# Writing out the loops of three engines, and laying high and low parts side by side, in a two-layer encoder step

## The chip, the cores and the metric

The kernel runs on one core of one Trainium2 chip. The metric is the device time of one launch in microseconds (us), taken as the median of several runs. A core has five engines with instruction streams of their own: TensorE (PE, matrix products; its weight loads are shown apart as PEld), VectorE (DVE), ScalarE (ACT), GpSimd (POOL) and SyncE (SP). They meet through semaphores. The work memory of a core has 128 partitions; products are summed up in PSUM, which has 8 banks here called `ps`.

## What is computed

Two layers for 288 rows of width 2048 (256 of a prompt, 32 of a sample with a past of 512). Each layer normalizes, projects, attends in two ways with 8 heads each, projects back, and ends with a squared-ReLU MLP whose hidden width is 8192. Cut to what matters:

```python
def trunk(x, caches_even, caches_odd):
    for i in range(DEPTH):                       # DEPTH = 2
        h = rms_norm(x, attn_norm[i])
        y, st = even_mixer(h, ...) if i % 2 == 0 else odd_mixer(h, ...)
        x = x + y
        x = x + squared_relu_mlp(rms_norm(x, mlp_norm[i]), w_up[i], w_down[i])

def squared_relu_mlp(h, w_up, w_down):
    return jnp.square(jax.nn.relu(h @ w_up)) @ w_down

def even_mixer(h, ...):
    aq, ak, av, iq, ik, iw, bq, bk, bv, bf = split_cols(h @ w_in, EVEN_SIZES)
    ...
    y = jnp.concatenate([out_a, out_b], axis=-1) @ w_out
```

All of it is in float32. The large products are with weights, 756 chunks of 512 KB of them in all, each read once.

## The kernel before

**Products in three.** A float32 product is made of products of a narrower type (fp32r). A weight chunk is split into `w_high` (a rounded copy, by ScalarE, line 784) and `w_low` (the rest, by VectorE, line 1063), an activation in the same way into `x_high` and `x_low`, or for the MLP's hidden values `hid_high_a`, `hid_low_a` (tiles 0 to 7) and `hid_high_b`, `hid_low_b` (tiles 8 to 15). TensorE then adds high times high (line 352), low activation times high weight (353) and high activation times low weight (354), each a 128x128 weight load and 288 moving columns, into one PSUM tile.

**Groups and chunks.** The weights come as one stream of 189 groups, each 2048 rows by 256 columns, cut into 4 chunks of 128x1024 (512 KB). A group is 96 such products, a chunk 24. The function `group` (from line 340) of TensorE waits per chunk for `low_ready`, and at the group's start for the evacuation of the bank used before. `raw` holds 4 chunks as they landed, `w_high` and `w_low` hold 2 each. For each chunk SyncE starts the load once VectorE has used the chunk 3 earlier; ScalarE makes `w_high` and VectorE `w_low` once TensorE has used the chunk 2 earlier. Between chunks, VectorE also empties the bank of the group before: times the norm factor into `proj` (line 1080), ReLU and square (1105, 1108) and the low part of the hidden values (1113) in an MLP's upper half, or added to `resid` (1124) in its lower half. ScalarE writes the high part of the hidden values (788).

**Order of the phases.** Input projection A (8 groups), a narrow group, projection B (12) with attention A beside it, output projection (16 groups of half length) with attention B beside it, MLP 0 (64 groups), projection C (12), projection D (12) with attention C beside it, output projection with attention D beside it, MLP 1 (64 groups). Work that stands beside attention has been written out in Python. The rest runs in hardware loops (`Fori`), whose bodies TensorE, ScalarE and VectorE pass through again by a branch:

- TensorE: `pairs` (line 388) has a body of two groups: 3 passes in projection A, 5 in projection C. `mlp` (line 411) writes quarter 0 out and has a body of one quarter, 16 groups (8 up, 8 down), for quarters 1 to 3: 3 passes per MLP.
- ScalarE: `plain` (817) one group per pass; projection A two groups (1016); the MLP's quarters 1 and 2 (1036, 1044), with 0 and 3 written out.
- VectorE: `phase_in` (1151) and projection A (1502) two groups; the MLP's quarters 1 and 2 (1531, 1542).

In a loop, the values that are waited for depend on the loop's counter, so register instructions stand between the others. I call the branch from a body's end back to its start a back edge. TensorE has four of a quarter (two per MLP) and six of two groups (two in projection A, four in projection C). SyncE's own loop over all groups stands in both kernels.

Of the kernel before, what the change touches and what calls it, by code (L numbers as in the profile page):

```python
# [11 lines left out]
F32R = mybir.dt.float32r  # L12


P = 128
# [6 lines left out]
H = 8  # L22
# [109 lines left out]
def build(nc, ins, outs):  # L132
    with ExitStack() as ctx:
# [16 lines left out]
        x_high = sb("x_high", [P, KT, T], F32R)  # L150
        x_low = sb("x_low", [P, KT, T], F32R)
# [7 lines left out]
        hid_high_a = sb("hid_high_a", [P, H, T], F32R)  # L159
        hid_low_a = sb("hid_low_a", [P, H, T], F32R)  # L160
# [136 lines left out]
        def _(pe):  # L297
# [84 lines left out]
            def pairs(base, count, moving, first_ready=None, apart=False, lead=0, window=None):  # L382
                group(base, base % 2, moving, ready=first_ready, apart=apart, lead=lead, window=window)
                if apart:

                    pe.wait_ge(mean_ready, 1)
                group(base + 1, (base + 1) % 2, moving, apart=apart, lead=lead)
                with pe.Fori(1, count // 2) as i:
                    group(base + i * 2, base % 2, moving, apart=apart, lead=lead)
                    group(base + 1 + i * 2, (base + 1) % 2, moving, apart=apart, lead=lead)  # L390
# [8 lines left out]
            def mlp(base, name, lead, i_norm):  # L399
# [11 lines left out]
                with pe.Fori(1, QUARTERS) as q:  # L411
                    quarter(q)
# [361 lines left out]
        def _(act):  # L774
# [40 lines left out]
            def plain(base, count, i_norm):  # L815
                body(base, i_norm=i_norm)
                with act.Fori(1, count) as i:
                    body(base + i)
# [197 lines left out]
            with act.Fori(1, IN_A // 2) as i:  # L1016
                for u in range(2):
                    body(i * 2 + u)
                    low_copy(i * 2 + u, u)
# [16 lines left out]
            with act.Fori(1, QUARTERS - 1) as q:  # L1036
                mlp_quarter(G_MLP0, E_OUT0, 0, q)
# [6 lines left out]
            with act.Fori(1, QUARTERS - 1) as q:  # L1044
                mlp_quarter(G_MLP1, E_OUT1, 1, q)
# [4 lines left out]
        def _(dve):  # L1050
# [97 lines left out]
            def phase_in(base, count, i_norm):  # L1148
                evac_in(base, base % 2, 0, i_norm)
                evac_in(base + 1, (base + 1) % 2, 2)  # L1150
                with dve.Fori(1, count // 2) as i:
                    evac_in(base + i * 2, base % 2, i * 4)
                    evac_in(base + i * 2 + 1, (base + 1) % 2, i * 4 + 2)
# [348 lines left out]
            with dve.Fori(1, IN_A // 2) as i:  # L1502
# [28 lines left out]
            with dve.Fori(1, QUARTERS - 1) as q:  # L1531
                quarter(G_MLP0, E_OUT0, 0, q)
# [9 lines left out]
            with dve.Fori(1, QUARTERS - 1) as q:  # L1542
# [295 lines left out]
```

How the kernel before makes its waits and increments, by code:

```python
        @block.sync  # L280
        def _(sp):
            w = ins["w"]
            for kk in range(CH):
                sp.dma_start(raw[:, kk, :], w[kk, :, :]).then_inc(landed[kk], 16)
                sp.dma_start(resid[:, CK * kk:CK * kk + CK, :], ins["x"][:, CK * kk:CK * kk + CK, :])\
                  .then_inc(x_landed[kk], 16)
            with sp.Fori(1, NG) as n:
                for kk in range(CH):
                    sp.wait_ge(low_ready, n * CH + (kk - 3))
                    sp.dma_start(raw[:, kk, :], w[bass.ds(n * CH + kk, 1), :, :].rearrange("a p c -> p (a c)"))\
                      .then_inc(landed[kk], 16)
# [10 lines left out]
            def out_pair(base, lead, half, j, window=None):  # L304
                e = base + lead + OUT_G * half + j
                pe.wait_ge(evacuated, e - 1)
                for i in range(HALF_CH):
                    c = base * CH + (OUT_G * half + j) * HALF_CH + i
                    pe.wait_ge(low_ready, c + 1)
# [14 lines left out]
            def out_half(base, lead, half, before, window=None, windows=0):  # L325
                pe.wait_ge(hid_low_ready, before)
                for j in range(OUT_G):
                    out_pair(base, lead, half, j, window)
                for w in range(OUT_WINDOWS, windows):
                    window(w)
# [28 lines left out]
            def sum_squares(i):  # L360
                pe.wait_ge(sum_ready, POOL_PAIRS + 8 * i)
                out = ps[:, 6 if i == 0 else 4, 0:T]
                if i == 0:
                    pe.wait_ge(sem("dim_squares"), 1)
```

## Time and profile before

| | us |
|---|---|
| median of 3 runs | 2697.96 |
| lowest and highest run | 2697.1, 2708.48 |
| span of the profiled execution | 2695.6 |
| TensorE busy | 2648.1 |
| VectorE busy | 1443.7 |
| ScalarE busy | 996.7 |

The span goes from the first to the last instruction of the profiled execution; its own time is not known apart, and the median lies 2.36 us above its span. In a timeline, a row of the view is its start, its duration, the engine, the line of the kernel, the operation, the tiles and, in brackets, how long the engine had been idle before and who ended that. Durations of products overlap, since they are pipelined: what counts is the distance from one start to the next. "issue" as the ender of an idle time means that nothing the profile shows was waited for.

### The profile page before, as it was taken

The numbers are of one execution on the slowest core, as the hardware profiler recorded it, in microseconds if no ns is written. First come the engines' busy times: TensorE is split into PE (matmuls) and PEld (weight loads), VectorE is DVE, ScalarE is ACT, GpSimd is POOL, SyncE is SP. The second block draws the span as 40 slices with busy tenths as digits, with TensorE's granted clock in tenths as the row PEclk, the third lists the DMA queues.
The fourth block names the chain that finished last, engine by engine and source line by source line (L and its number), as shares of the span: only waits on it lengthen the run. The fifth ranks groups of instructions, "written<-read, shape, count | busy, mean of one in ns | idle before, by whom it ended". The sixth has DMA issues, their size and how long they took to land.

```text
span 2695.6 us, 48256 instructions
## 1 busy us (share of the span) xinstructions
PE 2648.1 (98%) x19365; PEld 2588.9 (96%) x19365; DVE 1443.7 (54%) x1630; ACT 996.7 (37%) x1233; POOL 172.8 (6%) x162
## 2 busy tenths in 40 slices
PE   7999999999999999999999999999999999999998
PEld 7989987999999999999999999999999999999998
DVE  6577753754454455455644553557544544544543
ACT  3343442433333333333333442434333333333332
POOL 2011110300000000000200000213000000000000
PEclk9999998999999999999999998999999999999999
DMA  5534432445444444445454543444545444544553
GB/s 203 168 132 166 151 125 94 145 165 168 164 164 165 164 165 164 165 165 164 162 195 166 173 158 129 165 143 157 166 167 168 165 164 157 168 167 154 168 179 132
DMA packets 116348, 431.35 MB, mean 160 GB/s; under 512 B 13936, under 2 KB 14272, under 8 KB 113856
## 3 DMA queue, kind: packets, MB, share of 16 engines
q1 hardware_dynamic: 109440, 398.77, 44.1%
q0 software_dynamic: 5664, 29.56, 3.1%
q8 instruction: 154, 2.52, 0.4%
q10 hardware_dynamic: 1056, 0.22, 0.0%
q14 instruction: 34, 0.28, 0.0%
HBM read 418.31 MB, written 10.11 MB: 159 GB/s over the span
## 4 chain that ended last, share of the span: by engine, by line
PE 96%; DVE 2%; issue 1%; ACT 1%; DMA 0%; SPq 0%; POOL 0%; DVEq 0%; ACTq 0%; POOLq 0%
PE ps L352 27%; PE ps L354 27%; PE ps L353 27%; PE ps L318 3%; PE ps L319 3%; PE ps L320 3%; PE ps L560 1%; PE ps L434 1%; PE ps L509 1%; PE ps L545 1%; PE ps L487 1%; DVE w_low L1063 0%; PE ps L722 0%; ACT w_high L784 0%; PE ps L562 0%
## 5 line engine op out<-in xcount | busy, mean ns | idle before, releaser
L1063 DVE TENSOR_TENSOR w_low<-raw,w_high 128x1024 fp32r<-128x1024 f32 x756 | 952.6, 1260 | 981.5 <-ACT w_high L784 979.2
L784 ACT CAST w_high<-raw 128x1024 fp32r<-128x1024 f32 x756 | 793.2, 1049 | 1491.1 <-PE ps L354 1377.1
L352 PE MATMUL ps<-x_high,w_high 128*128 128x288 f32 x3472 | 1041.3, 300 | 27.1 <-DVE x_low L1132 15.5
L354 PE MATMUL ps<-x_high,w_low 128*128 128x288 f32 x3472 | 1028.9, 296 | 0.0
L353 PE MATMUL ps<-x_low,w_high 128*128 128x288 f32 x3472 | 1028.7, 296 | 0.0
L352 PEld LDWEIGHTS ps<-x_high,w_high 128*128 128x128 f32 x3472 | 655.9, 189 | 34.4 <-issue 24.7
L353 PEld LDWEIGHTS ps<-x_low,w_high 128*128 128x128 f32 x3472 | 656.4, 189 | 3.0 <-issue 2.4
L354 PEld LDWEIGHTS ps<-x_high,w_low 128*128 128x128 f32 x3472 | 655.8, 189 | 0.1
L352 PE MATMUL ps<-hid_high_a,w_high 128*128 128x288 f32 x1024 | 302.8, 296 | 0.0
L354 PE MATMUL ps<-hid_high_a,w_low 128*128 128x288 f32 x1024 | 302.2, 295 | 0.0
L354 PE MATMUL ps<-hid_high_b,w_low 128*128 128x288 f32 x1024 | 302.2, 295 | 0.0
L352 PE MATMUL ps<-hid_high_b,w_high 128*128 128x288 f32 x1024 | 302.1, 295 | 0.0
L353 PE MATMUL ps<-hid_low_a,w_high 128*128 128x288 f32 x1024 | 302.0, 295 | 0.0
L353 PE MATMUL ps<-hid_low_b,w_high 128*128 128x288 f32 x1024 | 302.0, 295 | 0.0
L352 PEld LDWEIGHTS ps<-hid_high_a,w_high 128*128 128x128 f32 x1024 | 192.2, 188 | 1.4 <-DVE w_low L1063 1.4
L353 PEld LDWEIGHTS ps<-hid_low_a,w_high 128*128 128x128 f32 x1024 | 192.3, 188 | 0.0
L353 PEld LDWEIGHTS ps<-hid_low_b,w_high 128*128 128x128 f32 x1024 | 192.3, 188 | 0.0
L354 PEld LDWEIGHTS ps<-hid_high_a,w_low 128*128 128x128 f32 x1024 | 192.3, 188 | 0.0
L354 PEld LDWEIGHTS ps<-hid_high_b,w_low 128*128 128x128 f32 x1024 | 192.2, 188 | 0.0
L352 PEld LDWEIGHTS ps<-hid_high_b,w_high 128*128 128x128 f32 x1024 | 192.2, 188 | 0.0
L318 PE MATMUL ps<-hid_high_a,w_high 128*128 128x288 f32 x256 | 81.9, 320 | 0.7 <-DVE hid_low_a L1272 0.7
L318 PE MATMUL ps<-hid_high_b,w_high 128*128 128x288 f32 x256 | 79.5, 311 | 1.4 <-DVE hid_low_b L1272 1.4
(316 smaller groups left out, 1984.9 us busy)
## 6 DMA issues: line engine op xcount, KB each, us to landing
raw<-in_w SPq DMA_DIRECT2D x756, 512.0 KB, 3.3
resid<-in_x SPq DMA_DIRECT2D x4, 576.0 KB, 8.0
out_y<-resid POOLq DMA_DIRECT2D x8, 288.0 KB, 2.5
scr<-in_k_past_B POOLq DMA_DIRECT2D x2, 1024.0 KB, 5.4
scr<-in_v_past_B POOLq DMA_DIRECT2D x2, 1024.0 KB, 6.2
scr<-in_k_past_C POOLq DMA_DIRECT2D x2, 1024.0 KB, 6.3
scr<-in_v_past_C POOLq DMA_DIRECT2D x2, 1024.0 KB, 8.0
scr<-in_k_past_D POOLq DMA_DIRECT2D x2, 1024.0 KB, 5.8
```

What stands on the lines that cost most here:

```text
L318: pe.matmul(out, wh, high, start=k % 8 == 0, stop=False)
L319: pe.matmul(out, wh, low, start=False, stop=False)
L320: last = pe.matmul(out, w_low[:, c % 2, at:at + P], high, start=False, stop=k % 8 == 7)
L352: pe.matmul(out, wh, high, start=k == 0, stop=end and apart)
L353: pe.matmul(out_low, wh, low, start=k == 0 and apart, stop=False)
L354: last = pe.matmul(out_low, w_low[:, kk % 2, at:at + rows], high, start=False, stop=end)
L434: last = pe.matmul(ps[:, b + u, 0:T], ones[:, :], pair_squares(ph, i)[:, u, :], start=True, stop=True)
L487: last = pe.matmul(ps[:, b, at:at + keys], queries, k[:, 0:keys], start=True, stop=ph != "B")
L509: pe.matmul(flat[32 * j:32 * j + 32, 2048:2048 + PAST], lhs, past, **flags)
L545: pe.matmul(ps[:, 7, 0:TP], v[:, 0, :], w[:, 0:TP], start=True, stop=False)
L784: act.copy(w_high[:, kk % 2, :], raw[:, kk, :]).then_inc(high_ready, 1)
L1063: dve.tensor_tensor(w_low[:, kk % 2, :], raw[:, kk, :], w_high[:, kk % 2, :].bitcast(F32), ALU.subtract)\
```

## The change

All the loops of TensorE, ScalarE and VectorE become Python loops, so that their instructions are written out one after the other with constants in the place of registers. SyncE's loop stays. `x_high` and `x_low` become two views of one tile in which each of the 16 blocks has its high 288 columns followed by its low 288; likewise `hid_high_a` and `hid_low_a`. The total size is the same, and every other tile stays at its address. No product, copy or transfer is added or removed, and every product still reads 288 columns side by side.

```diff
-        x_high = sb("x_high", [P, KT, T], F32R)
-        x_low = sb("x_low", [P, KT, T], F32R)
+        x_parts = sb("x_parts", [P, KT, 2, T], F32R)
+        x_high, x_low = x_parts[:, :, 0, :], x_parts[:, :, 1, :]
...
-        hid_high_a = sb("hid_high_a", [P, H, T], F32R)
-        hid_low_a = sb("hid_low_a", [P, H, T], F32R)
+        hid_parts_a = sb("hid_parts_a", [P, H, 2, T], F32R)
+        hid_high_a, hid_low_a = hid_parts_a[:, :, 0, :], hid_parts_a[:, :, 1, :]
...
                 group(base + 1, (base + 1) % 2, moving, apart=apart, lead=lead)
-                with pe.Fori(1, count // 2) as i:
+                for i in range(1, count // 2):
                     group(base + i * 2, base % 2, moving, apart=apart, lead=lead)
                     group(base + 1 + i * 2, (base + 1) % 2, moving, apart=apart, lead=lead)
...
                 quarter(0, first=True)
-                with pe.Fori(1, QUARTERS) as q:
+                for q in range(1, QUARTERS):
                     quarter(q)
...
             mlp_quarter(G_MLP0, E_OUT0, 0, 0, i_norm=1)
-            with act.Fori(1, QUARTERS - 1) as q:
+            for q in range(1, QUARTERS - 1):
                 mlp_quarter(G_MLP0, E_OUT0, 0, q)
...
             quarter(G_MLP0, E_OUT0, 0, 0, i_norm=1)
-            with dve.Fori(1, QUARTERS - 1) as q:
+            for q in range(1, QUARTERS - 1):
                 quarter(G_MLP0, E_OUT0, 0, q)
```

The other loops (lines 817, 1016, 1044, 1151, 1502, 1542) are changed in the same way.

Program order on TensorE in MLP 0, before, at the end of the loop's body (line 411): behind the quarter's last product come a register instruction and the branch; what follows the branch in the program is reached after the third pass only.

```order
L354 MATMUL ps<-hid_high_b,w_low 128x288
L411 REGISTER_ALU
L411 COMPARE_AND_BRANCH
L352 MATMUL ps<-x_high,w_high 128x288 [waits low_ready,x_low_ready,banks_evacuated]
L353 MATMUL ps<-x_low,w_high 128x288
L354 MATMUL ps<-x_high,w_low 128x288
```

The same engine and place after the change, between quarters 1 and 2.

```order
L352 MATMUL ps<-hid_high_b,w_high 128x288
L353 MATMUL ps<-hid_low_b,w_high 128x288
L354 MATMUL ps<-hid_high_b,w_low 128x288
L352 MATMUL ps<-x_parts,w_high 128x288 [waits low_ready,banks_evacuated]
L353 MATMUL ps<-x_parts,w_high 128x288
L354 MATMUL ps<-x_parts,w_low 128x288
```

The register instruction and the branch are gone, and the next quarter's first product follows. TensorE's program grows from 11590 to 18687 such rows.

Program order on VectorE at the end of its loop's body in MLP 0 (line 1531), before.

```order
L1124 TENSOR_TENSOR resid<-resid,ps 128x576 [waits chunk_used]
L1060 REGISTER_ALU
L1063 TENSOR_TENSOR w_low<-raw,w_high 128x1024 [waits chunk_used,high_ready]
L1531 REGISTER_ALU
L1531 COMPARE_AND_BRANCH
```

The same engine after the change, between two quarters.

```order
L1124 TENSOR_TENSOR resid<-resid,ps 128x576 [waits chunk_used]
L1063 TENSOR_TENSOR w_low<-raw,w_high 128x1024 [waits chunk_used,high_ready] x4
L1105 SCALAR_TENSOR_TENSOR tmp<-ps,rinv 128x576 [waits chunk_used]
L1108 TENSOR_TENSOR tmp<-tmp 128x576 [waits banks_evacuated]
L1063 TENSOR_TENSOR w_low<-raw,w_high 128x1024 [waits chunk_used,high_ready]
L1113 TENSOR_TENSOR hid_parts_a<-tmp,hid_parts_a 128x2x288 [waits hid_high_ready,squared]
```

Here too the registers and the branch are gone; the computing instructions keep their order. The write of two hidden tiles is now two pieces of 288 with a gap between them (128x2x288).

## Rows read from the trace of the kernel before

**Rows 1.** The page: span; busy time of each engine; granted clock in 40 slices

```profile
span 2695.6 us, 48256 instructions
PE 2648.1 (98%) x19365; PEld 2588.9 (96%) x19365; DVE 1443.7 (54%) x1630; ACT 996.7 (37%) x1233; POOL 172.8 (6%) x162
PEclk9999998999999999999999998999999999999999
```

**Rows 2.** Straight (540) and looped (940) stretch: busy by engine, clock, DMA share

```profile
540.00:720.00 180.00, 180.00 (x1358) 180.00 (x1357) 89.75 (x86) 64.24 (x65) 0.00 (x0) 1.00 0.50 164
940.00:1130.00 190.00, 190.00 (x1433) 190.00 (x1432) 94.68 (x91) 68.15 (x68) 0.00 (x0) 1.00 0.49 164
```

**Rows 3.** Waits of TensorE's weight loads, whole span: total us, times, longest

```profile
PEld ps L352 <- issue: 24.7, 17, 12.5
...
PEld ps L352 <- DVE w_low L1063: 5.4, 14, 1.2
```

**Rows 4.** Timeline of weight loads around the four back edges of a quarter

```profile
932.51 0.19 PEld L354 LDWEIGHTS ps<-hid_high_b,w_low 128*128 128x128 f32 x1
934.46 0.19 PEld L352 LDWEIGHTS ps<-x_high,w_high 128*128 128x128 f32 x1 [1.76 <-issue]
...
1138.25 0.19 PEld L354 LDWEIGHTS ps<-hid_high_b,w_low 128*128 128x128 f32 x1
1140.23 0.19 PEld L352 LDWEIGHTS ps<-x_high,w_high 128*128 128x128 f32 x1 [1.80 <-issue]
...
2271.57 0.19 PEld L354 LDWEIGHTS ps<-hid_high_b,w_low 128*128 128x128 f32 x1
2274.19 0.19 PEld L352 LDWEIGHTS ps<-x_high,w_high 128*128 128x128 f32 x1 [2.43 <-issue]
...
2478.15 0.19 PEld L354 LDWEIGHTS ps<-hid_high_b,w_low 128*128 128x128 f32 x1
2480.68 0.29 PEld L352 LDWEIGHTS ps<-x_high,w_high 128*128 128x128 f32 x1 [2.35 <-issue]
```

**Rows 5.** Weight loads at a two-group back edge (74) and from quarter 0 (728)

```profile
74.04 0.19 PEld L354 LDWEIGHTS ps<-x_high,w_low 128*128 128x128 f32 x1
74.18 0.19 PEld L352 LDWEIGHTS ps<-x_high,w_high 128*128 128x128 f32 x1
...
728.57 0.19 PEld L354 LDWEIGHTS ps<-hid_high_b,w_low 128*128 128x128 f32 x1
728.70 0.19 PEld L352 LDWEIGHTS ps<-x_high,w_high 128*128 128x128 f32 x1
```

**Rows 6.** Timeline, products and VectorE, around the first back edge of a quarter

```profile
932.98 0.75 DVE L1124 TENSOR_TENSOR resid<-resid,ps 128x576 f32<-128x576 f32 x1 [0.79 <-PE ps L354]
934.11 1.23 DVE L1063 TENSOR_TENSOR w_low<-raw,w_high 128x1024 fp32r<-128x1024 f32 x1 [0.38 <-ACT w_high L784]
934.47 0.40 PE L352 MATMUL ps<-x_high,w_high 128*128 128x288 f32 x1 [1.53 <-DVE resid L1124]
```

**Rows 7.** Stretch behind the last back edge, and the product that ends it

```profile
2481.00:2484.00 3.00, 3.00 (x14) 3.00 (x14) 0.00 (x0) 0.00 (x0) 0.00 (x0) 0.50 0.58 173
...
2484.18 0.29 PE L354 MATMUL ps<-x_high,w_low 128*128 128x288 f32 x1
```

**Rows 8.** The page's costliest groups: line, engine, tiles, count, busy, mean ns

```profile
L353 PE MATMUL ps<-x_low,w_high 128*128 128x288 f32 x3472 | 1028.7, 296 | 0.0
L353 PE MATMUL ps<-hid_low_b,w_high 128*128 128x288 f32 x1024 | 302.0, 295 | 0.0
L1063 DVE TENSOR_TENSOR w_low<-raw,w_high 128x1024 fp32r<-128x1024 f32 x756 | 952.6, 1260 | 981.5 <-ACT w_high L784 979.2
```

**Rows 9.** Groups of VectorE: one reads two PSUM banks, one reads a packed tile

```profile
L1105 DVE SCALAR_TENSOR_TENSOR tmp<-ps,rinv 128x576 f32<-128x576 f32 x64 | 48.5, 758 | 51.1 <-PE ps L354 51.1
L1108 DVE TENSOR_TENSOR tmp<-tmp 128x576 f32<-128x576 f32 x64 | 48.5, 758 | 2.2
```

**Rows 10.** The page's DMA queues: packets, MB, share of 16 engines

```profile
q8 instruction: 154, 2.52, 0.4%
```

More of the change, by code:

```diff
@@ L816, in plain @@
                 body(base, i_norm=i_norm)
-                with act.Fori(1, count) as i:
+                for i in range(1, count):
                     body(base + i)
@@ L1015, in _ @@
             low_copy(1, 1)
-            with act.Fori(1, IN_A // 2) as i:
+            for i in range(1, IN_A // 2):
                 for u in range(2):
@@ L1043, in _ @@
             mlp_quarter(G_MLP1, E_OUT1, 1, 0, i_norm=3)
-            with act.Fori(1, QUARTERS - 1) as q:
+            for q in range(1, QUARTERS - 1):
                 mlp_quarter(G_MLP1, E_OUT1, 1, q)
@@ L1150, in phase_in @@
                 evac_in(base + 1, (base + 1) % 2, 2)
-                with dve.Fori(1, count // 2) as i:
+                for i in range(1, count // 2):
                     evac_in(base + i * 2, base % 2, i * 4)
@@ L1501, in _ @@
                 evac_apart(n, n % 2, proj[:, 2 * n:2 * n + 2, :], first=n == 0)
-            with dve.Fori(1, IN_A // 2) as i:
+            for i in range(1, IN_A // 2):
                 evac_apart(i * 2, 0, proj[:, bass.ds(i * 4, 2), :])
@@ L1530, in _ @@
             quarter(G_MLP0, E_OUT0, 0, 0, i_norm=1)
-            with dve.Fori(1, QUARTERS - 1) as q:
+            for q in range(1, QUARTERS - 1):
                 quarter(G_MLP0, E_OUT0, 0, q)
@@ L1541, in _ @@
             quarter(G_MLP1, E_OUT1, 1, 0, i_norm=3)
-            with dve.Fori(1, QUARTERS - 1) as q:
+            for q in range(1, QUARTERS - 1):
                 quarter(G_MLP1, E_OUT1, 1, q)
```

## The prediction, made before the changed kernel ran

> **What bounds the kernel now.** I read the page first: TensorE is busy for 2648.1 of 2695.6 us, VectorE for 54% and ScalarE for 37% of the span [rows 1]. A busy engine here is one that issues products back to back, so the next question is how fast it does. The stretches answer it: in quarter 0 of MLP 0, which is written out already, 1358 products take 180 us, 132.6 ns each; in the middle of quarter 2, which is a pass of a loop, 1433 take 190 us, again 132.6 ns [rows 2]. TensorE is never idle in either, at a granted clock of 1.00, the higher level of 2.4 GHz. So the body of a loop runs no slower than straight code, and the register instructions between its products cost nothing that can be seen. What the change can win on TensorE lies in the few places where it does not issue. The waits of the weight loads name them: 24.7 us in 17 places behind "issue", where nothing in the profile was waited for, of which 12.5 us is one gap at the start [rows 3].
>
> I then looked in the timeline for every distance between two weight loads of the large products that is over 0.5 us, where 0.13 us is usual. In the looped stretches there are only four, and they are the four back edges of a quarter [rows 4]. The two-group back edges show nothing: 74.04 to 74.18 us is the usual distance [rows 5], and the other five look the same.
>
> **The change part by part: the four long back edges.** The distances from the last load of a quarter to the first of the next are 1.95, 1.98, 2.62 and 2.53 us [rows 4]. Less the 0.13 us that would pass anyway, 1.82 + 1.85 + 2.49 + 2.40 = 8.56 us. Behind the last one there is more. For 2481 to 2484 us the granted clock is 0.50, the lower level of 1.2 GHz, after TensorE had stood still for 2.4 us; 14 distances between products, from the first at 2480.69 to the one at 2484.18, take 3.49 us where 14 x 0.1326 = 1.86 us is usual [rows 7]. That is 1.63 us more. The other three gaps were not followed by such a fall. Sum: 8.56 + 1.63 = 10.19 us.
>
> Is it the branch that makes these gaps? The row at 934.47 puts the wait down to VectorE's addition to `resid`, but that ended at 932.98 + 0.75 = 933.73 us, 0.74 us earlier [rows 6]. And the passage from quarter 0 to quarter 1, at 728.57 to 728.70 us, has the same work on both sides and the same evacuation, but no branch back, and takes 0.13 us [rows 5]. So the gap goes with the long way back in the program and not with the boundary between quarters. Once written out, all seven boundaries of this kind look like that one.
>
> What is late next when the gap goes? The second chunk of the new quarter. Its `w_low` ends at 934.11 + 1.23 = 935.34 us [rows 6]. Without the gap TensorE would begin the quarter at 932.64 us and want that chunk 24 x 0.1326 = 3.18 us later, at 935.82 us: 0.48 us of cover. VectorE's and ScalarE's own back edges fall on the same moments in two of the four places (from quarter 1 to 2) and there the gap is no longer than in the others (1.95 and 1.98 us in MLP 0), so they hide in it, and they go away too. If they should leave VectorE 1 us late, it would cost 0.5 us per place.
>
> On the size of a back edge the Trainium skill has two rules that disagree. "Advanced Engine Details and Errata", section Control Flow Timing, gives a compare-and-branch about 108 ns; by that alone, an estimate from that page, the ten back edges would be worth at most 1.1 us and the median would come to 2696.9 us. "Runtime: NRT & Kernel Launch", section Instruction fetch mechanics, says that a taken branch whose target is outside the window of instructions held stalls for a fetch; by that the long bodies stall and short ones need not, which is what the rows above show, so the trace sides with this one, and the first page's figure has its place beside the rival of the gap that stays.
>
> **The register instructions and the short loops.** They cost nothing in the rows (132.6 ns in both stretches), so I put their removal at nothing. The bounds: 0.05 ns per product, the rounding of that comparison, over the 10752 products in loops is 0.5 us either way. The loops of VectorE and ScalarE are covered by TensorE: it is busy for the whole of the looped stretch while they work half and a third of it [rows 2]. If shorter waits in them also took away TensorE's waits for `w_low`, that would be 5.4 us at the very most [rows 3]; but the larger of them, of up to 1.2 us, stand at the narrow group, where nobody loops, and the others, of 0.2 us, in quarter 3 of MLP 0, where VectorE and ScalarE don't loop. So I take nothing.
>
> **The layout.** A product still streams 288 adjacent columns; only the address differs. Tiles at quite different addresses take the same time: `x_low` 296 ns and `hid_low_b` 295 ns in the mean [rows 8]. VectorE and ScalarE now write and read two hidden tiles with a gap between the pieces. The nearest rows: an operation that reads two PSUM banks, pieces of 288 out of 512, takes 758 ns, and one on a packed tile of the same size takes 758 ns too [rows 9]. So nothing; and from both sides, if each product changed by 0.1 ns (a thirtieth of a per cent of a duration, below what the rows resolve), it would be 1.8 us over 18144 products either way.
>
> **Straight code must be fetched.** A queue for instructions moved 154 packets and 2.52 MB before the change [rows 10]. The program of TensorE grows from 11590 to 18687 rows, but the number of instructions that run does not, and quarter 0, straight code already, has no gap in 180 us [rows 2]. So I put that at nothing too.
>
> The sum: 2695.6 - 10.2 = 2685.4 us of span, and with the 2.36 us by which the median stands above it, 2687.8 us. That is 0.38% less. About 0.5%, or 13.5 us, is what a measurement of this kernel can tell from no change, so my forecast is "within 0.5%", on the faster side.
>
> **The rivals.**
>
> *The gap stays.* The boundary between quarters could need its 2 us for a reason I don't see, a fetch that comes late wherever TensorE's program is, say. For it: the row that names VectorE's `resid`. Against: quarter 0's boundary. Time: 2697.96 us, or some 2698.
>
> *More comes back than the gaps.* For it: `w_low` waits of 5.4 us [rows 3], and the granted clock, which fell once behind a gap and falls in the attention of the second layer too (the slice marked 8 at 1617 to 1685 us [rows 1]); everything from 934 us on now comes 2 to 4 us earlier, and a fall or two may not happen. A fall costs some 1.6 us, as behind the last gap. All 5.4 us and one fall: 2687.8 - 7.0 = 2680.8 us, which is 0.6% less. Against: the waits stand where the two engines' code is straight already, and falls may as well be added.
>
> *Written-out code is fetched late.* TensorE would come to the end of what has been fetched, and stand still, in stretches that used to be loops. The price here: the former loops run 112 groups of 96 products, 10752 of 19365 and as many weight loads, 56% of all; of 154 packets that is 86. If each brought the shortest of the four gaps, 1.82 us, the kernel would lose 157 us; from 0.12 us per packet on, the 10.2 us are eaten up, and from 0.28 us on the kernel is over 0.5% slower than before. With a stall of 0.3 us in each, 2687.8 + 25.8 = 2713.6 us. Against: quarter 0 runs 1358 products and as many loads as straight code without one such stall. The section of the Trainium skill's "Runtime: NRT & Kernel Launch" named above also says that the cost of crossing from one block of instructions to the next is "mostly hidden".
>
> *The layout slows products.* From 10.2 us / 18144 = 0.56 ns per product it would eat the gain. Nothing in the rows speaks for it beyond the fact that they show no tile laid out so. With 1 ns, 2706 us.
>
> **How the numbers follow.** The forecast of 2687.8 us gets 0.70; more comes back 0.14; the gap stays 0.07; late fetch 0.05; slower products 0.04. The forecast's own range is 2684 to 2692 us: 1.6 us per clock fall, in either direction, 0.5 us per boundary, 0.5 and 1.8 us of bounds, and a median of before that may itself be off by 1 us (runs of 2697.1 and 2697.96). The range of 8 in 10 must take in most of the two nearest cases, 2680.8 and 2698: 2681 to 2698 us. Faster by over 0.5% means below 2684.5 us: the 0.14 and a twelfth of the forecast's own, 0.20. Slower by over 0.5% means above 2711.5 us: most of the late fetch and a little of the layout, 0.06. Within: 0.74.
>
> **What would show it.** In the profile after: distances of 0.13 us at all boundaries of quarters, no granted clock of 0.50 behind quarter 2 of MLP 1, 132.6 ns per product in every stretch of the MLPs, durations of 295 to 296 ns, and the same 154 packets on the instruction queue, give or take. What would prove me wrong: gaps at new places on TensorE in an MLP, or a distance of products that has moved.

## The result, and the profile after

The changed kernel takes 2681.4 us in the median of 6 runs (2674.0 to 2684.64), beside 2700.64 us for the kernel before in 6 runs (2697.1 to 2708.48). The ratio is 0.9926, 95% interval 0.9906 to 0.9946. The whole interval lies beyond the 0.5% up to which I had called it no change: the change saves about 0.74%, and I had forecast 0.38%. The direction was right; the forecast was half the size.

The page of the kernel after: span, busy time of the engines, instruction queue.

```profile
span 2678.0 us, 47174 instructions
PE 2639.0 (99%) x19365; PEld 2580.8 (96%) x19365; DVE 1443.2 (54%) x1630; ACT 996.6 (37%) x1233; POOL 173.2 (6%) x162
q8 instruction: 152, 2.49, 0.4%
```

The span is 17.6 us shorter than in [rows 1]. VectorE and ScalarE are busy for as long as before, and the instruction queue moves about as much as in [rows 10]. TensorE's idle time falls from 47.5 to 39.0 us, and its busy time falls too, by 9.1 us for the same number of products. I had not expected that.

First the gaps. The timeline of weight loads in the kernel after, at the four places of [rows 4]:

```profile
929.49 0.19 PEld L354 LDWEIGHTS ps<-hid_high_b,w_low 128*128 128x128 f32 x1
929.62 0.19 PEld L352 LDWEIGHTS ps<-x_parts,w_high 128*128 128x128 f32 x1
...
1132.80 0.19 PEld L354 LDWEIGHTS ps<-hid_high_b,w_low 128*128 128x128 f32 x1
1132.93 0.19 PEld L352 LDWEIGHTS ps<-x_parts,w_high 128*128 128x128 f32 x1
...
2261.79 0.19 PEld L354 LDWEIGHTS ps<-hid_high_b,w_low 128*128 128x128 f32 x1
2261.92 0.19 PEld L352 LDWEIGHTS ps<-x_parts,w_high 128*128 128x128 f32 x1
...
2465.10 0.19 PEld L354 LDWEIGHTS ps<-hid_high_b,w_low 128*128 128x128 f32 x1
2465.23 0.19 PEld L352 LDWEIGHTS ps<-x_parts,w_high 128*128 128x128 f32 x1
```

All four distances are 0.13 us. The gaps are gone, and so is the stretch at the lower clock [rows 7].

Then the pace. The same stretches as in [rows 2] (the second is 6 us earlier, since everything is), with the same columns:

```profile
540.00:720.00 180.00, 180.00 (x1362) 180.00 (x1361) 89.78 (x85) 63.84 (x64) 0.00 (x0) 1.00 0.50 167
934.00:1124.00 190.00, 190.00 (x1438) 190.00 (x1437) 95.55 (x91) 67.81 (x69) 0.00 (x0) 1.00 0.50 166
```

There are 1362 products in 180 us where there were 1358, and 1438 in 190 us where there were 1433, at the same clock of 1.00. The first of these stretches was straight code in both kernels. So it is not the loops that quicken the products there.

For a finer measure I take the eight upper groups of a quarter, 768 products in a row: from the first weight load on an x tile to the first on a hidden tile. I call it the x stretch, and what follows, up to the next quarter, the hidden stretch, also 768 products. Timeline rows for quarter 1 of MLP 0, the kernel before (the x stretch begins at 728.70, [rows 5]), then the kernel after:

```profile
830.67 0.19 PEld L352 LDWEIGHTS ps<-hid_high_a,w_high 128*128 128x128 f32 x1
```

```profile
726.32 0.19 PEld L352 LDWEIGHTS ps<-x_parts,w_high 128*128 128x128 f32 x1
...
827.87 0.19 PEld L352 LDWEIGHTS ps<-hid_parts_a,w_high 128*128 128x128 f32 x1
```

The x stretch takes 101.97 us before and 101.55 after; in the five other quarters 1 to 3 of the kernel after it is 101.55 as well. The hidden stretch after is 929.62 - 827.87 = 101.75 us. Before, without the gap, it is 932.64 - 830.67 = 101.97. In these two kernels the stretches of one kind differ by no more than 0.03 us while the clock is at 1.00 and no wait falls into them, so they tell layouts apart with a single profile, where whole runs scatter by 10 us. (Behind the gap at 2271.57 us the x stretch before takes 102.12 us, since TensorE waits once more there: the distance of two loads is 0.31 us, 20 products on.)

**The account.** At the end of quarter 0 of MLP 0 the kernel after is 2.38 us ahead, after quarter 1 it is 4.84, after quarter 2 7.30 us. Of each 2.46 us, 0.42 + 0.21 = 0.63 belong to the two stretches and 1.83 to the gap. In the same way MLP 1 gives 2.50, 2.55 and 1.51 us besides the stretches. So the back edges gave 1.83 + 1.83 + 2.50 + 2.55 + 1.51 = 10.22 us. The other 7.4 us of the 17.6 are not all the layout's. Some 5.7 us come step by step in projections A and C and in the MLPs, all at a clock of 1.00, and those are the layout's, as the runs below show. But 1.4 us stand at the start: the 97th load on x comes at 35.96 us before and at 34.58 us after, because the clock was at its lower level there for longer in the profile of before. Before, then after:

```profile
20.00:27.00 7.00, 6.36 (x28) 6.36 (x29) 5.16 (x10) 0.67 (x3) 4.61 (x8) 0.53 0.46 147
20.00:27.00 7.00, 6.60 (x38) 6.60 (x39) 5.38 (x11) 2.11 (x4) 4.37 (x8) 0.76 0.51 160
```

The remaining 0.3 us came in the phases beside attention.

### The profile page after: what moved, and what is told of

Read it like the earlier page. It is cut to its first block, busy times and chain, and to the rows that moved or that the text cites. A ratio compares the mean times of both kernels' runs of the same rounds, so it can differ in the third digit from the quotient of the medians.

```text
span 2678.0 us, 47174 instructions
## 1 busy us (share of the span) xinstructions
PE 2639.0 (99%) x19365; PEld 2580.8 (96%) x19365; DVE 1443.2 (54%) x1630; ACT 996.6 (37%) x1233; POOL 173.2 (6%) x162
## 3 DMA queue, kind: packets, MB, share of 16 engines
q8 instruction: 152, 2.49, 0.4%
## 4 chain that ended last, share of the span: by engine, by line
PE 96%; DVE 1%; issue 1%; ACT 1%; DMA 0%; SPq 0%; POOL 0%; DVEq 0%; ACTq 0%; POOLq 0%
PE ps L352 27%; PE ps L354 27%; PE ps L353 27%; PE ps L318 3%; PE ps L319 3%; PE ps L320 3%; PE ps L560 1%; PE ps L434 1%; PE ps L509 1%; PE ps L545 1%; PE ps L487 1%; DVE w_low L1063 0%; ACT w_high L784 0%; PE ps L722 0%; PE ps L562 0%
## 5 line engine op out<-in xcount | busy, mean ns | idle before, releaser
L352 PE MATMUL ps<-x_parts,w_high 128*128 128x288 f32 x3472 | 1041.0, 300 | 18.5 <-DVE x_parts L1132 14.5
L353 PE MATMUL ps<-x_parts,w_high 128*128 128x288 f32 x3472 | 1025.1, 295 | 0.0
L354 PE MATMUL ps<-x_parts,w_low 128*128 128x288 f32 x3472 | 1023.4, 295 | 0.0
L352 PEld LDWEIGHTS ps<-x_parts,w_high 128*128 128x128 f32 x3472 | 653.8, 188 | 25.0 <-issue 16.0
L353 PEld LDWEIGHTS ps<-x_parts,w_high 128*128 128x128 f32 x3472 | 659.0, 190 | 3.0 <-issue 2.4
L354 PEld LDWEIGHTS ps<-x_parts,w_low 128*128 128x128 f32 x3472 | 657.9, 189 | 0.0
L352 PE MATMUL ps<-hid_parts_a,w_high 128*128 128x288 f32 x1024 | 303.1, 296 | 0.0
L353 PE MATMUL ps<-hid_parts_a,w_high 128*128 128x288 f32 x1024 | 301.2, 294 | 0.0
L354 PE MATMUL ps<-hid_parts_a,w_low 128*128 128x288 f32 x1024 | 300.8, 294 | 0.0
L353 PEld LDWEIGHTS ps<-hid_parts_a,w_high 128*128 128x128 f32 x1024 | 193.5, 189 | 0.0
L352 PEld LDWEIGHTS ps<-hid_parts_a,w_high 128*128 128x128 f32 x1024 | 191.9, 187 | 1.5 <-DVE w_low L1063 1.5
L354 PEld LDWEIGHTS ps<-hid_parts_a,w_low 128*128 128x128 f32 x1024 | 193.3, 189 | 0.0
L318 PE MATMUL ps<-hid_parts_a,w_high 128*128 128x288 f32 x256 | 82.0, 320 | 0.7 <-DVE hid_parts_a L1272 0.7
```

What stands on the lines that cost most here:

```text
L318: pe.matmul(out, wh, high, start=k % 8 == 0, stop=False)
L352: pe.matmul(out, wh, high, start=k == 0, stop=end and apart)
L353: pe.matmul(out_low, wh, low, start=k == 0 and apart, stop=False)
L354: last = pe.matmul(out_low, w_low[:, kk % 2, at:at + rows], high, start=False, stop=end)
```

## The experiments

Times of the experiments are medians, and each ratio is to runs of the kernel before taken beside them. A diff is against the changed kernel unless it says otherwise.

### Which part gave what: loops alone, layout alone

The first puts the old layout back into the changed kernel, the second puts the new layout into the kernel before.

```diff
-        x_parts = sb("x_parts", [P, KT, 2, T], F32R)
-        x_high, x_low = x_parts[:, :, 0, :], x_parts[:, :, 1, :]
+        x_high = sb("x_high", [P, KT, T], F32R)
+        x_low = sb("x_low", [P, KT, T], F32R)
...
```

> The loops of all three engines written out, the tiles laid out as before the change. My theory now: the change has two parts that add up, and this is the first. It should give the back edges alone: about 10 us of span less than before (8.56 us of gaps, 1.6 us of low clock), a ratio near 0.996, and distances between products as before, 132.3 ns from high times high to low times high on the x tiles. Rival: writing out also makes the products follow each other faster, and then the whole 0.7% (ratio 0.993) and 130.8 ns come here.

> High and low side by side, the loops kept. My theory: 130.8 ns instead of 132.3 ns from line 352 to line 353 on the x tiles (3472 pairs) and 131.3 instead of 132.5 on the hid_a tiles (1280 pairs), so 5.2 + 1.5 = some 7 us less, ratio near 0.9975, with four gaps of 2 to 2.6 us left at the back edges of a quarter. Rival: layout does nothing without the loops written out; ratio 1.000 and 132.3 ns.

Loops alone: 2685.99 us, ratio 0.9948 (0.9930 to 0.9966). Layout alone: 2694.12 us, ratio 0.9973 (0.9959 to 0.9987). The product of the two is 0.9921, the change's own 0.9926: the parts add up. Timeline rows of the kernel with the loops written out alone, the x stretch of quarter 1:

```profile
728.78 0.19 PEld L352 LDWEIGHTS ps<-x_high,w_high 128*128 128x128 f32 x1
...
830.75 0.19 PEld L352 LDWEIGHTS ps<-hid_high_a,w_high 128*128 128x128 f32 x1
```

101.97 us, as before the change: written-out code doesn't quicken the products. The kernel with the layout alone, the same stretch and one of its back edges, and below it the stretch behind that edge:

```profile
728.63 0.19 PEld L352 LDWEIGHTS ps<-x_parts,w_high 128*128 128x128 f32 x1
...
830.18 0.19 PEld L352 LDWEIGHTS ps<-hid_parts_a,w_high 128*128 128x128 f32 x1
```

```profile
1140.00:1143.00 3.00, 3.00 (x16) 3.00 (x15) 0.00 (x0) 0.00 (x0) 0.00 (x0) 0.56 0.55 176
```

101.55 us with loops in place, and four gaps of 2.01, 2.68, 2.41 and 2.25 us from load to load, the clock falling to 0.56 in the mean behind the second. Both rivals fall. A long back edge can cost a second, smaller wait: behind the third and the fourth gap, 20 products on, two loads are 0.64 and 0.45 us apart with the clock at 1.00. The row behind the third:

```profile
2277.10 0.19 PEld L354 LDWEIGHTS ps<-x_parts,w_low 128*128 128x128 f32 x1 [0.45 <-issue]
```

In all, such a second wait follows four of the twelve long back edges that were profiled.

### Which engine's branch makes the gap, and how long the body must be

```diff
-                for q in range(1, QUARTERS):
+                with pe.Fori(1, QUARTERS) as q:
                     quarter(q)
```

> The changed kernel, with one loop put back: TensorE's loop over quarters 1 to 3 in the two MLPs. ScalarE and VectorE stay written out. If TensorE's branch back makes the gaps, all four are there again, 1.9 to 2.6 us each, and 8.5 to 10 us come back: ratio to before near 0.9965. Rival: the gaps came from VectorE's and ScalarE's own branches, or only where all three branch: then none or only two gaps, at most 5 us.

2694.19 us, ratio 0.9977 (0.9961 to 0.9992). The four distances are 2.49, 2.57, 2.19 and 2.11 us, with ScalarE and VectorE written out. Timeline rows at the first, and the stretches behind the first and the second (columns as in [rows 2]):

```profile
925.10 0.19 PEld L354 LDWEIGHTS ps<-hid_high_b,w_low 128*128 128x128 f32 x1
927.59 0.19 PEld L352 LDWEIGHTS ps<-x_parts,w_high 128*128 128x128 f32 x1 [2.30 <-issue]
```

```profile
928.00:931.00 3.00, 3.00 (x17) 3.00 (x17) 0.00 (x0) 0.00 (x0) 0.00 (x0) 0.62 0.58 178
1135.00:1138.00 3.00, 3.00 (x23) 3.00 (x24) 0.13 (x1) 0.00 (x0) 0.00 (x0) 1.00 0.59 184
```

So it is TensorE's branch and nobody else's. The time came back more than I expected (0.9965, just inside the interval): less 0.13 us each the gaps are 8.8 us, and the clock fell behind two of them, the first and the third, where the x stretch that follows took 103.09 us instead of 101.55. Gaps and falls make 11.9 us, and the medians lie 12.8 us apart; the two profiled executions lie only 7.4 us apart, so other stages were shorter in this one.

The other experiment has many short back edges in the place of four long ones; the first two lower groups stay straight between its loops:

```diff
-                for q in range(1, QUARTERS):
-                    quarter(q)
+                for q in range(1, QUARTERS):
+                    with pe.Fori(0, 4) as i:
+                        for u in range(2):
+                            group(base + q * QG + u + i * 2, (base + u) % 2, X, lead=lead)
...
+                    with pe.Fori(1, 4) as i:
+                        for u in range(2):
+                            group(base + q * QG + 8 + u + i * 2, (base + u) % 2, HID, lead=lead)
```

> The changed kernel, with TensorE's quarters 1 to 3 of each MLP as short loops: 4 passes over two upper groups, then two groups straight, then 3 passes over two lower groups; 30 back edges in all instead of none. If a branch back over two groups costs nothing, as in the projections before the change, no distance over 0.2 us appears and the time is the changed kernel's, ratio near 0.993. Rival: each costs the 0.11 us of the Trainium skill's page Advanced Engine Details and Errata, 3.3 us in all, ratio 0.9945, or about 2 us each like the long ones, 60 us, ratio 1.015.

2679.92 us, ratio 0.9934 (0.9914 to 0.9955): the changed kernel's time. Timeline rows at its first back edge, 192 products behind 728.30 us, and the instruction queue of its page:

```profile
753.56 0.19 PEld L354 LDWEIGHTS ps<-x_parts,w_low 128*128 128x128 f32 x1
753.69 0.19 PEld L352 LDWEIGHTS ps<-x_parts,w_high 128*128 128x128 f32 x1
```

```profile
q8 instruction: 108, 1.77, 0.3%
```

The distances at the 30 short back edges are 0.132 to 0.136 us. The queue fits: 108 packets instead of 152, so the 30 repeated passes over two groups were not fetched again. The long loop goes the other way: 163 packets, 11 more than straight code, some 2.8 for each long back edge. That these are packets fetched ahead of the branch and thrown away is my reading; no row shows it. A body of 192 products stays with the engine, one of 1536 is fetched anew, and TensorE stands still for 2 to 2.6 us. The Trainium skill's "Runtime: NRT & Kernel Launch", section Instruction fetch mechanics, says that a taken branch out of the window of instructions held must wait for a fetch; gaps and packets here agree. The 108 ns that the Trainium skill's "Advanced Engine Details and Errata", section Control Flow Timing, gives for a compare-and-branch is not visible in this kernel: at none of the 30 is the distance over 0.136 us.

### What in the layout quickens the products

My first idea was nearness, or that one reading begins where the last ended. The mean distance from line 352 to line 353, worked out over 3400 pairs on x tiles, had fallen from 132.3 to 130.8 ns, while the next two stayed. Two kernels were to tell. One keeps the low part of x block k behind the high block k+1 (VectorE writes it there), the other puts low in front of high, in the x tiles (shown) and in the first hidden ones.

```diff
-                return x_high[:, k, :], x_low[:, k, :]
+                return x_high[:, k, :], x_low[:, (k + 1) % KT, :]
```

```diff
-        x_high, x_low = x_parts[:, :, 0, :], x_parts[:, :, 1, :]
+        x_low, x_high = x_parts[:, :, 0, :], x_parts[:, :, 1, :]
```

> The changed kernel, but the low part of x block k is kept in the place behind high block k+1, so that high k and low k are near (3456 bytes from start to start) but no longer end to start. hid_a stays side by side. If it is nearness that makes the second product of a pair start earlier, the x pairs stay at 130.8 ns. If it is that the second reading begins at the address where the first ended, they go back to 132.3 ns, and 5.2 us of span come back, ratio to before near 0.9945.

> The changed kernel with low in front of high inside each pair of tiles. Products keep their order: high x high, low x high, high x low. If adjacency forward is what counts, line 352 to 353 goes back to 132.3 to 132.5 ns and line 353 to 354 (low, then the high right behind it in memory) becomes the short one, 131.3 ns instead of 132.9; the total stays at the changed kernel's, ratio near 0.993. If it is about two products sharing one weight block and near data, 352 to 353 stays short at 130.8 ns and 353 to 354 at 132.9.

Near but apart: 2680.42 us, ratio 0.9933 (0.9911 to 0.9955), x stretch 101.55 us. Adjacency falls. Low first: 2670.9 us, 0.9901 (0.9879 to 0.9923), x stretch 101.55, hidden stretch 101.54 instead of 101.75 us. In it the pair 352 to 353 stayed short (131.1 ns), but 353 to 354 went up to 134.4 and 354 to 352 down to 130.1. So a single distance says little, since a delay shows at one product or the next; from here on I read whole stretches. That median is some 8 us below the changed kernel's 2681.4 less the 2.1 us that the stretches explain; the profiled run has a mean granted clock of 0.989 where the changed kernel's has 0.986, and what raised it is open. And the x tiles in it do not have one pace. One of its six x stretches took 2149.51 - 2048.81 = 100.70 us, 131.1 ns per product, and nearly all of projection C ran at that pace too, with the same tiles at the same addresses as in the stretches of 101.55 us:

```profile
2048.81 0.19 PEld L352 LDWEIGHTS ps<-x_parts,w_high 128*128 128x128 f32 x1
...
2149.51 0.19 PEld L352 LDWEIGHTS ps<-hid_parts_a,w_high 128*128 128x128 f32 x1
```

The addresses alone do not fix the pace, then.

In all these layouts, side by side or near, the step from high to low is an odd multiple of 128 bytes, since a block is 1152 = 9 x 128 bytes. Before the change it was 18432 = 72 x 256. The next kernels separate that from nearness. Far apart, but with the low tile 128 bytes later:

```diff
+        x_high = sb("x_high", [P, KT, T], F32R)
+        x_low_room = sb("x_low_room", [P, KT * T + 128], F32R)
+        x_low = x_low_room[:, 32:32 + KT * T].rearrange("p (k t) -> p k t", k=KT)
```

and near, but with an even step: high k, high k+1, low k, low k+1, so 2304 = 9 x 256 bytes.

```diff
+        x_parts = sb("x_parts", [P, KT // 2, 2, 2, T], F32R)
+        x_high, x_low = x_parts[:, :, 0, :, :], x_parts[:, :, 1, :, :]
```

> Loops written out; x_high and x_low in two separate tiles as before the change, but the low one begins 128 bytes later, so that low k lies some 18560 bytes behind high k instead of 18432; hid_a as before the change. Two theories for what made the pair 352 to 353 short. Nearness: the tiles are as far apart as ever, so 132.6 ns and the total of the loops-only kernel, ratio near 0.995. Address step: with tiles of 1152 bytes, side by side also meant that high and low differ by an odd multiple of 128 bytes, and that is kept here; then x pairs take 131 ns, 4 us of span less than the loops-only kernel, ratio near 0.993.

> Loops written out; the x tile holds high k, high k+1, low k, low k+1 one behind the other, so that low k is 2304 bytes behind high k: near, but an even multiple of 128 bytes, a multiple of 256, as before the change. hid_a side by side as in the changed kernel. Nearness: x pairs at 131 ns, ratio near 0.993. Address step: x pairs back at 132.6 ns, ratio near 0.9945.

Far and shifted: 2673.28 us, ratio 0.9906 (0.9884 to 0.9928). Near and even: 2685.39 us, 0.9947 (0.9931 to 0.9963). Their x stretches, first the far and shifted one, then the near and even one:

```profile
723.62 0.19 PEld L353 LDWEIGHTS ps<-x_high,w_high 128*128 128x128 f32 x1
...
824.75 0.19 PEld L353 LDWEIGHTS ps<-hid_high_a,w_high 128*128 128x128 f32 x1
```

```profile
725.16 0.19 PEld L352 LDWEIGHTS ps<-x_parts,w_high 128*128 128x128 f32 x1
...
827.13 0.19 PEld L352 LDWEIGHTS ps<-hid_parts_a,w_high 128*128 128x128 f32 x1
```

101.13 us and 101.97 us. Nearness is out: these near tiles gain nothing, and the far ones gain twice what the change gained. What is left is the step's remainder to 256 bytes, or the place of the tiles.

Two more kernels were to get more out of the first idea, before it had fallen. One lays the second eight hidden tiles out low first too (and the attention tiles `k_bd` and `v_bd`, which share their memory, likewise). The other changes the order of products in a chunk:

```diff
-                    for k2 in range(CK):
-                        k = kk * CK + k2
-                        high, low = moving(k)
-                        for f in range(tiles):
...
+                    for f in range(tiles):
...
+                        for k2 in range(CK):
...
+                            pe.matmul(out_low, w_low[:, kk % 2, at:at + rows], high, start=k == 0, stop=False)
+                            pe.matmul(out, wh, high, start=k == 0 and apart, stop=end and apart)
+                            last = pe.matmul(out_low, wh, low, start=False, stop=end)
```

> The kernel with low in front of high, with the second eight hidden tiles laid out in the same way (low first; they share memory with two attention tiles, which are interleaved alike). The other eight gave 398.2 to 395.2 ns per three products between the kernel before and the low-first kernel; the same for the 1280 threes of hid_b is 3.5 to 3.8 us less than low-first, ratio near 0.989. Rival: the interleaved attention tiles cost VectorE and TensorE as much, same time as low-first.

> The changed kernel with the products of a chunk in another order: for each of the two column tiles all four k blocks in turn, and inside each, high x low weight first, then high x high, then low x high. So each step goes on to the next address or stays, seven times of eight. Nearness or forward adjacency: more steps are short, 394 ns or less per three products instead of 396.7, some 10 us less than the changed kernel, ratio near 0.989. If the step between addresses mod 256 bytes decides and not the order, the threes stay at 396 to 398 ns and the ratio at 0.993.

Low first on all tiles: 2670.89 us, ratio 0.9885 (0.9861 to 0.9909), hidden stretch 101.55 us, so nothing beyond low first on the first eight (101.54). But that sum hides two changes: the second eight gained 0.19 us per stretch, and the first eight, whose addresses had not changed, lost as much. With low first on them alone, half of their groups ran at 131.2 ns and half at 132.2; now all run at 132.2. The other order: 2680.66 us, 0.9931 (0.9910 to 0.9951), x stretch 101.58 us, hidden stretch 102.16. It gains nothing, and loses 0.4 us in the hidden stretch.

### The step or the place, and how small a step

> As the kernel with x_low 128 bytes later, but 64 bytes later. What counts in the shift? If any offset from a multiple of 256 does, the x stretch of 768 products takes 101.12 us again; if it must be an odd multiple of 128, it takes 101.97 us as before the change and the ratio is the loops-only kernel's, 0.995.

> Loops written out, x_high and x_low in far tiles again and both 64 bytes later than before the change, so that the step between them is 18432 bytes as before while each stands 64 bytes off. hid_a as before. Read: the x stretch of 768 products. If the step between high and low decides, it takes 101.97 us as before the change. If the place of the tiles decides, 101.12 us as with only the low one moved.

> Loops written out, the low tile in front and the high tile 18560 bytes behind it, so that the step has the same size as in the kernel with x_low 128 bytes later but the high blocks are the moved ones. By the step alone 101.12 us for the x stretch. If it matters which of the two stands at an odd multiple of 128 bytes, something between 101.12 and 101.97 us.

> As the kernels with x_low 128 and 64 bytes later, but 16 bytes later. If any step that is no multiple of 256 bytes will do, 101.12 us for the x stretch; if a coarser unit (64 bytes) counts, 101.97 us.

> Loops written out, x tiles side by side as in the changed kernel, the whole pair 64 bytes later; hid_a as before the change. Step by step the same as the changed kernel, so by the step alone 101.55 us for the x stretch. If the half gain of side by side (101.55 instead of 101.12) comes from where the blocks stand, it changes, to 101.12 or 101.97 us.

The edits are like this one, of the run with both tiles moved by 16 floats; with 16 bytes, the high tile has 0 in the place of 16 and the low one 4:

```diff
+        x_room = sb("x_room", [P, 2 * KT * T + 128], F32R)
+        x_high = x_room[:, 16:16 + KT * T].rearrange("p (k t) -> p k t", k=KT)
+        x_low = x_room[:, KT * T + 16:KT * T + 16 + KT * T].rearrange("p (k t) -> p k t", k=KT)
```

Timeline rows of the x stretch: both moved by 64 bytes, then low moved by 16 bytes, then side by side moved by 64 bytes.

```profile
721.79 0.19 PEld L353 LDWEIGHTS ps<-x_room,w_high 128*128 128x128 f32 x1
...
823.76 0.19 PEld L353 LDWEIGHTS ps<-hid_high_a,w_high 128*128 128x128 f32 x1
```

```profile
733.50 0.19 PEld L353 LDWEIGHTS ps<-x_room,w_high 128*128 128x128 f32 x1
...
834.62 0.19 PEld L353 LDWEIGHTS ps<-hid_high_a,w_high 128*128 128x128 f32 x1
```

```profile
729.07 0.19 PEld L353 LDWEIGHTS ps<-x_room,w_high 128*128 128x128 f32 x1
...
831.46 0.19 PEld L353 LDWEIGHTS ps<-hid_high_a,w_high 128*128 128x128 f32 x1
```

The last columns are worked out from the same weight loads over groups of 96 products, in other phases that read the same x tiles: projection A and quarter 0 of both MLPs, and projection C.

| layout of the x tiles | bytes from high k to low k | x stretch, us | ns per product | A and quarter 0, ns | C, ns |
|---|---|---|---|---|---|
| before, and loops alone | 18432 | 101.97 | 132.8 | 132.8 | 132.8 |
| pairs of two | 2304 | 101.97 | 132.8 | 132.8 | 132.8 |
| both tiles 64 later | 18432 | 101.97 | 132.8 | 132.2 | 132.8 |
| side by side (the change) | 1152 | 101.55 | 132.2 | 132.2 | 132.2 |
| near apart | 3456 | 101.55 | 132.2 | 132.2 | 132.2 |
| low first, side by side | -1152 | 101.55 | 132.2 | 132.2 | 131.1 |
| side by side, 64 later | 1152 | 102.39 | 133.3 | 133.3 | 133.3 |
| low 128 later | 18560 | 101.13 | 131.7 | 131.7 | 131.7 |
| low 64 later | 18496 | 101.12 | 131.7 | 131.7 | 132.2 |
| low 16 later | 18448 | 101.12 | 131.7 | 133.9 | 131.7 |
| low tile in front | -18560 | 101.12 | 131.7 | 131.7 | 131.7 |

By the x stretch alone, far tiles follow a simple rule: with a step of 18432 bytes a product takes 1.1 ns longer than with any other of the four steps tried, and moving both tiles changes nothing. The other phases break that rule. Rows of quarter 0 and quarter 1 of MLP 0, first both tiles 64 later, then low 16 later (columns as in [rows 2]; 605 products in 80 us before the change in either place):

```profile
540.00:620.00 80.00, 80.00 (x607) 80.00 (x607) 43.18 (x44) 30.27 (x31) 0.00 (x0) 1.00 0.49 165
740.00:820.00 80.00, 80.00 (x605) 80.00 (x604) 43.52 (x44) 30.23 (x31) 0.00 (x0) 1.00 0.50 167
```

```profile
540.00:620.00 80.00, 80.00 (x599) 80.00 (x598) 44.01 (x45) 30.25 (x31) 0.00 (x0) 1.00 0.47 160
740.00:820.00 80.00, 80.00 (x609) 80.00 (x609) 43.19 (x43) 31.07 (x32) 0.00 (x0) 1.00 0.50 166
```

With both tiles moved the step is as before, and yet quarter 0 is faster than before; with 16 bytes quarter 0 is slower than before, by 1.1 ns per product, while quarter 1 is faster by as much. So neither the step nor the addresses decide by themselves; something that differs between the phases has a part, and what it is, is open. With tiles side by side the step fails too: the same pair 64 bytes later has every step between x blocks as in the change and takes 102.39 us, worse than before the change. Nor do the runs show that 256 bytes is the unit: 18432 is a multiple of 512, 1024 and 2048 as well, and only the near kernel of pairs, with 2304, speaks for 256. What is shown is that the place of the tiles changes the pace, and that the change's own layout has 132.2 ns in all these phases where the old one has 132.8.

Four of these kernels were run once only: 2679.57 us with both moved, 2675.05 with the low tile in front, 2686.03 with 16 bytes and 2691.11 with side by side moved, beside 2697.49 us for the kernel before. Low 64 later has 2675.51 us, ratio 0.9912 (0.9892 to 0.9933).

### A kernel that beats both

All low tiles 128 bytes later: x, and both halves of the hidden tiles, with `k_bd`, which shares memory with `hid_low_b`, moved likewise.

```diff
+        low_room_b = sb("low_room_b", [P, H * T + 128], F32R)
+        hid_low_b = low_room_b[:, 32:32 + H * T].rearrange("p (h t) -> p h t", h=H)
+        hid_high_a = sb("hid_high_a", [P, H, T], F32R)
+        low_room_a = sb("low_room_a", [P, H * T + 128], F32R)
+        hid_low_a = low_room_a[:, 32:32 + H * T].rearrange("p (h t) -> p h t", h=H)
```

> Loops written out, high and low in separate tiles, and in all three pairs (x, hid_a, hid_b) the low tile begins 128 bytes later. In the kernel with only the x tile shifted, 768 products on x took 101.12 us instead of 101.97, and those on hidden tiles 101.96 as before. If the step between addresses decides, the hidden stretches also come to 101.12 us: 1.1 ns for each of 18096 large products, 20 us less than the loops-only kernel, median near 2667, ratio 0.987 to 0.989. Rival: side by side has a merit of its own, then hidden stretches stay near 102.

2666.38 us, ratio 0.9881 (0.9860 to 0.9902). Its stretches in quarter 1:

```profile
724.45 0.19 PEld L356 LDWEIGHTS ps<-x_high,w_high 128*128 128x128 f32 x1
...
825.57 0.19 PEld L356 LDWEIGHTS ps<-hid_high_a,w_high 128*128 128x128 f32 x1
...
926.69 0.19 PEld L356 LDWEIGHTS ps<-x_high,w_high 128*128 128x128 f32 x1
```

101.12 us and 101.12 us: the hidden tiles gain what the x tiles gain, and with 128 bytes quarter 0 and the projections A and C have 131.7 ns too. It costs 1.5 KB of each partition and no instruction. Its median is 19.6 us below that of the loops-only kernel (18 us by the two ratios), where 18096 x 1.11 ns = 20.1 us were worked out.

## Why the prediction was right and wrong

**What bounds the kernel: right.** TensorE's issue sets the time, and only what changed that showed in the result. VectorE and ScalarE are busy for the same time, and nothing came of their loops.

**The four long back edges: right, and closer than the working deserved.** The sum said 8.56 us of gaps and 1.63 us of low clock, 10.19 in all. The account of the two traces gives 10.22 us. That they agree to 0.03 us is luck: two small errors cancel. The gap was read from load to load and the low clock from product to product, which counts 0.12 us twice; read from the loads, the stretch behind the fall is 103.48 - 101.97 = 1.51 us longer. And the second wait behind the third gap, 0.15 us, was missed. The reasons held as well: the gap is the branch's and not the boundary's, it is TensorE's own, the short loops have none, and the chunk behind the boundary came in time. But the fall of the clock behind the last one was a draw, not a property of that place: behind twelve such gaps in three profiled kernels (before, layout alone, TensorE's loop put back) it fell four times, at different ones.

**Registers and straight code: right.** The stretch takes 101.97 us in the looped and the written-out kernel alike, and late fetch of straight code had no part. The instruction queue moved 152 packets where I had said 154, but that agreement is luck too. By the experiments, an estimate, four long back edges add 11 packets and six short ones save 6 x 44 / 30 = 8.8, which nearly cancels in the kernel before.

**The layout: wrong, and this is the step that failed.** I wrote "So nothing", with 1.8 us either way as bounds. It is 0.42 us per 768 products on x and 0.21 us per 384 on the first hidden tiles; over 10416 and 3840 products that is 5.7 + 2.1 = 7.8 us, and the traces leave 7.4 us beside the back edges, of which 1.4 us is the clock at the start. The layout alone measured 0.27% less, some 7 us. Three faults are in that step. The rows I rested on, 296 and 295 ns for tiles "at quite different addresses" [rows 8], were durations of overlapping products, which I had said myself tell nothing of the pace. Both pairs had steps of a multiple of 256 bytes, 18432 and 9216, and both ran at 132.8 ns, so the two together could not have shown the effect. And the bound of 0.1 ns per product came from no row; 18096 times an unseen nanosecond, 18 us, is over half a per cent of this kernel, so an unknown of that kind wanted a far wider bound. My rival on the layout considered only that it slows products.

**The total.** With the layout's 7.8 us, the same sum gives 2695.6 - 10.2 - 7.8 = 2677.6 us of span; 2678.0 was measured, with the help of the clock at the start. The 2.36 us from span to median are not a property of the kernel: each execution's own time lies 1.8 us above its span (2679.78 beside 2678.0), and the rest is scatter between runs. I had given 0.20 to a gain over 0.5%, but for waits for `w_low` and falls of the clock; the waits are 5.6 us in the kernel after where they were 5.4. So the measured 2681.4 us lies inside my range of 8 in 10, 2681 to 2698 us, for a reason that I had not thought of.

## What to carry to other kernels

Where an engine issues the same kind of product thousands of times, a nanosecond in its pace is worth more than all the gaps one can see; measure it as the time of a long unbroken stretch, and try tiles that stand a few bytes off. Take stretches in several phases: the 16 bytes that looked as good as 128 in one stretch were slower than nothing done in another. In this kernel 128 bytes between far tiles gained in every phase looked at; side by side moved by 64 bytes lost in all. Write out TensorE's long loops, or cut them into short ones; short loops run as fast as straight code and are fetched less.

## What the runs showed of the hardware that I had not expected

- The pace of 128x288 products with a 128x128 weight load each changes with the place of the moving tiles. Seen were 131.1, 131.7, 132.2, 132.8, 133.3 and 133.9 ns, some 0.55 ns from one to the next. One layout can have two of them in one execution: 132.2 and 131.1 ns with low first, 133.9 and 131.7 with low 16 bytes later.
- TensorE keeps a body of 192 products and their loads: 30 repeated passes saved 44 packets of the instruction queue (108 instead of 152), while four long back edges took 11 more (163).
- Behind a long back edge, 1.9 to 2.7 us from load to load, the granted clock fell to the lower level of 1.2 GHz in four of twelve cases and stayed at 2.4 GHz in the others; the gap's length didn't decide it (2.19 us with a fall, 2.62 and 2.57 us without). A fall costs 1.5 us here (x stretches of 103.48 instead of 101.97 us, and 103.09 instead of 101.55).
- The scatter of whole runs goes with the clock: runs of the kernel before have spans of 2690.0 us at a mean granted clock of 0.988 up to 2708.6 us at 0.980. At one clock, 0.986, the spans are 2692 to 2694 us before, 2678.0 after, 2684 to 2686 with the loops alone.
